# Splitting three multi-part steps of a merged attention and DeltaNet stage

## The reference, cut to what matters

```
# head group A, causal attention, 8 heads, then a norm over the 512 outputs of a token
s = qn . k_nope + qp . k_pe, scaled, causal mask
p = softmax(s)
o = p @ v ;  y_mla = o * rsqrt(mean(o*o) + EPS) * out_norm
# head group B, gated DeltaNet, 4 heads, chunked
lower  = strict_lower(k_beta @ k.T * decay)
sol    = triangular_solve(lower + I, [v_beta | k_beta * exp(g)])
a_qk   = causal(q @ k.T * decay)
v_new  = u_c - w_c @ state ; o_c = q_dec @ state + a_qk @ v_new
state  = state * exp(g_last) + k_dec.T @ v_new
```

## Time and profile before

| what | value |
|---|---|
| median of 3 runs | 2585.17 us (2581.58 to 2592.66) |
| the profiled execution, its own time | 2578.27 us |
| span in its trace | 2576.6 us |
| PE, PEld busy | 2331.9, 1339.2 us |
| DVE, ACT, POOL busy | 1074.2, 910.1, 392.4 us |
| mean granted TensorE clock | 0.949 of full speed |

### The profile page before, as it was taken

One profiled execution on the slowest core, in us unless ns is written; L12 is line 12 of the kernel. 1 busy time (PEld: TensorE's weight loads), 2 busy tenths in 40 slices (PEclk: granted clock), 3 DMA queues, 4 the chain that ended last, 5 costly groups with the idle time before them and its releaser, 6 DMA issues. The chain is left out here.

```text
span 2576.6 us, 47589 instructions
## 1 busy us (share of the span) xinstructions
PE 2331.9 (91%) x17494; PEld 1339.2 (52%) x17495; DVE 1074.2 (42%) x2440; ACT 910.1 (35%) x2283; POOL 392.4 (15%) x630
## 2 busy tenths in 40 slices
PE   6999999999688999999999999699985999999990
PEld 2545545455356666666666667355543444444440
DVE  2433334333345665665666566224345222222223
ACT  2263462734545554554545554111110011010112
POOL 1000000000110000000000010133321222222224
PEclk8999999999879999999999999899987999999995
DMA  9112121110353213121221112833321879999787
GB/s 335 72 65 70 52 78 54 56 54 32 107 141 105 75 53 94 56 82 49 80 69 65 51 33 95 294 126 111 131 90 33 238 193 307 273 323 303 225 237 287
DMA packets 187896, 334.49 MB, mean 130 GB/s; under 512 B 19724, under 2 KB 119719, under 8 KB 184503
## 3 DMA queue, kind: packets, MB, share of 16 engines
q1 hardware_dynamic: 173878, 281.51, 32.3%
q0 software_dynamic: 13824, 50.34, 8.1%
HBM read 242.36 MB, written 89.44 MB: 129 GB/s over the span
## 5 line engine op out<-in xcount | busy, mean ns | idle before, releaser
L706 PE MATMUL pV<-mod_rows_then_work,w_in_sb 128*128 128x512 f32 x768 | 341.3, 598 | 4.7 <-DMA w_in_sb<-in_w_in_dram 4.7
L2066 PE MATMUL hidden_ps<-w,keys_values_then_all 128*128 x752 | 331.5, 594 | 1.0 <-SPq L1938 1.0
L1140 ACT ACTIVATE probs<-scores,neg_max 128x512 f32<-128x512 f32 (+3 forms) x320 | 199.5, 624 | 345.6 <-DVE neg_max L1265 228.5
L1417 PE MATMUL scores<-keys_values_then_all,queries 96*128 96x512 f32 (+3 forms) x640 | 309.9, 567 | 7.2 <-DMA keys_values_then_all<-kp_d 7.2
L706 PEld LDWEIGHTS pV<-mod_rows_then_work,w_in_sb 128*128 128x128 f32 x768 | 145.0, 191 | 178.2 <-issue 177.5
L2066 PEld LDWEIGHTS hidden_ps<-w,keys_values_then_all 128*128 128x128 f32 x752 | 143.2, 191 | 181.5 <-issue 181.5
L1715 PE MATMUL out_ps<-keys_values_then_all 128*128 128x512 f32 x512 | 226.2, 600 | 2.5 <-ACT keys_values_then_all L1580 2.5
L1422 PE MATMUL bank<-ident,probs 128*128 128x128 f32 x1088 | 188.7, 290 | 7.0 <-ACT probs L1140 6.7
L1265 DVE TENSOR_REDUCE neg_max<-scores 128x1 f32<-128x512 f32 x192 | 132.2, 688 | 131.7 <-PE scores L1417 131.1
L1434 PE MATMUL outT_ps<-probs_T,keys_values_then_all 128*64 128x128 f32 x2176 | 160.0, 287 | 27.3 <-issue 23.1
L1996 ACT ACTIVATE keys_values_then_all<-hidden_ps 128x256 f32<-128x256 f32 x47 | 18.0, 384 | 455.5 <-PE hidden_ps L2066 455.5
(11 more groups left out here) (368 smaller groups left out, 3317.3 us busy)
## 6 DMA issues: line engine op xcount, KB each, us to landing
w<-in_w_dram SPq DMA_DIRECT2D x64, 1024.0 KB, 10.3
w_sb<-in_w_dram SPq DMA_DIRECT2D x32, 1024.0 KB, 14.4
w_mod_rows<-in_w_mod_dram SPq DMA_DIRECT2D x16, 1024.0 KB, 5.0
kqv<-qkv_d SPq DMA_DIRECT2D x16, 768.0 KB, 4.3
mod_rows_then_work<-in_w_mod_dram SPq DMA_DIRECT2D x4, 2048.0 KB, 14.9
x_in<-in_x_dram SPq DMA_DIRECT2D x16, 512.0 KB, 4.2
qkv_d<-l_out SPq DMA_DIRECT2D x32, 256.0 KB, 2.3
keys_values_then_all<-y_d SPq DMA_DIRECT2D x16, 512.0 KB, 4.9
```

The lines of the kernel that those rows point to most:

```text
L706: last = pe.matmul(pV[n % 2][:], win[:, k, QKV0 + c * P:QKV0 + (c + 1) * P], hT[:, s % 2, k, :], start=(k == 0), stop=(k == ND - 1))
L1140: act.activation(prob[:, e, 0:w].rearrange("p t k -> p (t k)"), pS[e][:, 0:w * P], ACT.Exp, scale=-1.0, bias=nmin[:, i % 2, h, b:b + 1], a ...
L1417: pe.matmul(pS[e][:, 0:w * P], qT[:, i % 2, slot(h)], kT[:, 4 * b:4 * b + w, slot(h), :], start=True, stop=True).then_inc(s_ready, 1)
L2066: last = pe.matmul(pH[par][:], xT[par][:, k], m.w13[:, ds(slot, 1), k].rearrange("p s n -> p (s n)"), start=(k == 0), stop=(k == ND - 1))
```

## The change

K's four parts on DVE and POOL become separate steps. Step K keeps the four operations that write `lt`. KA follows. U0 then makes `xt[:, 0]` directly from the diagonal blocks of `lt`, by four operations of 32 partitions in place of one of 128 on the compact copy, and then the first U. A new step KB has the compact copy and, on POOL, the other four masks. U0 cost 0.0 in the spacing and K with KA 1.7; now K, KA, U0 and KB cost 2.5.

B keeps the minimum and the gaps. Its exponential is step BX and its four last operations are step B2, placed in the next tile's first pair: BX behind the first head's X, B2 behind the second head's. A keeps the square (and POOL's part). The scaling and SP's store are step AS: one pair later where the next tile has more than 4 pairs, which is so for 12 of the 16 tiles, else directly behind A.

```
@@ mix_order: atoms
+            if i and (i, hp, b) == (i, 0, 0):
+                atoms.append((0.0, [(("BX", "B2")[e], i - 1, 0)]))
...
             atoms.append((0.0, [("B", i, 0)]))
+        if i and o == (AH // 2 if TILE[i] >= 4 else AH // 2 - 1):
+            atoms.append((0.0, [("AS", i - 1, 0)]))
+    atoms.append((0.0, [("BX", NT - 1, 0), ("B2", NT - 1, 0)]))
...
@@ mix_order: steps
-        steps += [(1.0, ("K", n)), (0.0, ("U0", n)), (0.7, ("KA", n))] * prep
+        steps += [(1.0, ("K", n)), (0.5, ("KA", n)), (0.5, ("U0", n)), (0.5, ("KB", n))] * prep
@@ SP
-                elif kind == "A":
+                elif kind == "AS":
                     wait(ya_ready, n + 1)
@@ POOL
-                elif kind == "K":
+                elif kind == "KB":
                     wait(ltb_ready, n + 1)
@@ ACT
-                elif kind == "B":
+                elif kind == "BX":
                     wait(gap_ready, n + 1)
...
                     act.activation(ya[:], att[:].rearrange("p h d -> p (h d)"), ACT.Square, accum_out=ass[:]).then_inc(asq_ready, 1)
+                elif kind == "AS":
                     wait(a_pow, 2 * n + 2)
@@ DVE
                 elif kind == "K":
                     wait(kk_ready, n + 1)
                     wait(em_ready, n + 1)
-                    wait(xt_ready, n)
                     wait(xw_ready, n * NLV)
...
                     last.then_inc(lt_ready, 1)
+                elif kind == "KB":
                     wait(lt_ready, n + 1)
+                    wait(xt_ready, n)
                     for q in quarter:
                         last = dve.tensor_copy(ltb[q], lt[q, :, q])
                     last.then_inc(ltb_ready, 1)
-                    wait(ltb_ready, n + 1)
-                    dve.tensor_tensor(xt[:, 0], ltb[:], mask_b[:, 0].unsqueeze(1).to_broadcast([P, GH, BL]), ALU.mult).then_inc(x0_ready, 1)
...
                 elif kind == "U0":
+                    wait(lt_ready, n + 1)
+                    for q in quarter:
+                        last = dve.tensor_tensor(xt[q, 0], lt[q, :, q], mask_b[q, 0].unsqueeze(1).to_broadcast([BL, GH, BL]), ALU.mult)
+                    last.then_inc(x0_ready, 1)
                     wait(x0_ready, n + 1)
...
+                elif kind == "B2":
+                    nb = TILE[n] // 4 + 1
                     wait(wexp_ready, n + 1)
```

More of the change, by code:

```diff
@@ L736, in mix_order @@
             atoms.append((0.0, [("B", i, 0)]))
+        if i and o == (AH // 2 if TILE[i] >= 4 else AH // 2 - 1):
+            atoms.append((0.0, [("AS", i - 1, 0)]))
+    atoms.append((0.0, [("BX", NT - 1, 0), ("B2", NT - 1, 0)]))
     for o in range(AH // 2):
         atoms.append((0.44, [("O", NT - 1, o)]))
-    atoms.append((0.0, [("A", NT - 1, 0)]))
+    atoms.append((0.0, [("A", NT - 1, 0), ("AS", NT - 1, 0)]))
     steps = []
@@ L760, in mix_order @@
         steps += [(0.9, ("Y", n, 6)), (0.5, ("WU", n, 6))] * prep
-    order = [("G", 0), ("K", 0), ("U0", 0), ("KA", 0), ("S", 0, 0), ("X", 0, 0), ("S", 0, 1), ("X", 0, 1)]
+    order = [("G", 0), ("K", 0), ("KA", 0), ("U0", 0), ("KB", 0), ("S", 0, 0), ("X", 0, 0), ("S", 0, 1), ("X", 0, 1)]
     steps = [(cost, step) for cost, step in steps if step not in order]
```

## The result

The changed kernel takes 2549.28 us (median of 6; 2543.02 to 2552.67) against 2587.46 for the kernel before beside it: ratio 0.9846, 95% interval 0.9832 to 0.9859. That is 38 us faster, where 14 had been forecast, and lies 1.3 us above the lower end of the range. The profiled execution has a span of 2543.2 us, against 2576.6.

What follows compares the result with a forecast made beforehand. PE was taken to wait on attention's round trip through in-order DVE and ACT queues, no engine being full. Terms -7.5 - 3.2 - 3.2 = -13.9 us, applied to the 2585.17 us median, gave 2571.3 us, range 2548 to 2592.

Steps and rivals of the forecast that it cites:

- What bounds the kernel: Merged stage, 909 us: no engine full by its own work; PE waits for attention's round trip through in-order DVE and ACT.
- Part A: Norm's scaling on ACT one pair later: six tiles in full, less a quarter, -7.5 us; bounds 0 and 20 us.
- Part B: Block weights on DVE: wait for ACT's small exponential nearly vanishes, 0.2 us a tile, -3.2 us; bounds 0 and 25.0.
- Part K: Gram step on DVE: earlier probs_T copy -8.0 us, longer second group +4.8, net -3.2; bounds -19 and +16 us.
- Spacing: DeltaNet steps weigh 18.25, not 17.45; inverse's round trips drawn closer, 2 us on 47.4 of waits, offset, set at zero.
- Most waits pass in full: Rival, merged stage: A 20, B 8 and K's first group 12 us, 40 us gained, 2545 us; chance 0.10.
- Absorbed: Rival: each removed wait uncovers another; half a gain at A, none at B and K, about 2581 us; chance 0.27.
- The slower rival: Gram step's longer second group delays row minima: +24 us against -8 from A and B, 2601 us; chance 0.13.

Runs made afterwards that it cites:

- extra copy behind the square: Changed kernel plus one unused 128x512 ACT copy directly behind the norm's square, 16 times: ratio 0.9890.
- extra matmuls: Kernel before plus unneeded PE matmuls where PE waits behind the norm, 12 tiles: 18 a tile, 2615.91 us; 6 a tile, 2592.5 us.
- the kernel where ACT still waits at the old place: Kernel before with only the norm's scaling one pair later, ACT still waiting for POOL's root directly behind the square: 2578.98 us, ratio 0.9947.
- the run with fewer extra matmuls: Kernel before plus 4 matmuls before V of the fifth pair and 2 before T of the sixth, in 12 tiles: 2592.5 us, ratio 1.0007.
- the old costs: Kernel before with only the Gram step split, K, KA, U0 and KB weighing 1.7 together in the spacing as before: 2566.71 us, ratio 0.9932.
- the spacing alone: Kernel before, nothing split, with K's cost in the spacing 1.5 and KA's 1.0 in place of 1.0 and 0.7: 2580.56 us, ratio 0.9966.

## Why the prediction was wrong, point by point

**What bounds the kernel** held. PE waits on attention's round trip, and what counts is which link stands behind what in an in-order queue.

**Part A is the step that failed.** The term read -7.5 us: six tiles in full, less a quarter for what PE waits for next. The mechanism, a backlog on ACT that ends at a load of PE, was right and its size was wrong: A alone brings 31 us, in company 21. I had two stretches, one that passed in full and one that didn't, and took half. The second of them, at the norm of 1101.8, is one of only two tiles of twelve that gain nothing: ten pass on 0.8 to 1.8 us each, 14.5 us of PE's idle time together, twice the term, and no next wait takes a quarter of it back. The term's upper bound, 20 us, is what A has in company; alone it has more than the ACT time it frees. The extra copy behind the square fits the full price (+11 us for 9.7), and the extra matmuls that PE took in for nothing show that the idle time is there.

**The clock** was missing from the sum altogether, and is likely most of the rest. In the kernel before, around the norm at 923.95, the granted clock was at its full level up to 929 and then fell from the upper of its two levels (2.4 GHz) to the lower (1.2 GHz) for most of the next 4 us. The same follows the norms at 969.1, 1171.8, 1331.2 and 1420.8, all of them tiles in which a load stood 2.0 to 3.3 us; behind the norm at 1036.0, where one stood 2.48 us, it didn't fall. The last row is the stretch behind the norm at 1171.8:

```profile
core 0: us, PE busy (x) PEld busy (x) DVE busy (x) ACT busy (x) POOL busy (x), PEclk, DMA share, GB/s
923.00:929.00 6.00, 3.56 (x43) 1.91 (x41) 3.68 (x10) 4.99 (x15) 1.63 (x3) 1.00 0.33 83
929.00:933.00 4.00, 4.00 (x31) 3.26 (x30) 0.11 (x1) 1.22 (x4) 0.00 (x0) 0.57 0.94 300
1175.00:1179.00 4.00, 4.00 (x19) 2.84 (x18) 1.45 (x3) 1.12 (x4) 0.00 (x0) 0.59 0.19 70
```

In the changed kernel the 9 to 11 us behind these five norms all have a granted clock of 1.00. At 929, PE's loads had stood 3.24 us ahead of the fall:

```profile
928.41 0.54 PEld L1364 LDWEIGHTS bank<-W_half,A_transposed 64*64 64x64 f32 x8 [3.24 <-issue]
929.01 1.52 PEld L1434 LDWEIGHTS outT_ps<-probs_T,keys_values_then_all 128*64 128x64 f32 x16
```

The same two groups of loads in the kernel with A alone:

```profile
923.11 0.54 PEld L1369 LDWEIGHTS bank<-W_half,A_transposed 64*64 64x64 f32 x8 [1.58 <-issue]
923.71 0.85 PEld L1439 LDWEIGHTS outT_ps<-probs_T,keys_values_then_all 128*64 128x64 f32 x16
```

V's 16 loads took 1.52 us behind the long wait and 0.85 us behind the shorter one. From 800 to 1560 us the mean granted clock is 0.97 before, 0.98 with A alone and 0.99 in the changed kernel. All kernels but the two with extra matmuls have the same 17,495 loads; with A's whole split they are busy 1329.6 to 1335.8 us (nine profiles, mean 1332.9), without it and with no matmuls added 1339.2 to 1345.3 (eight, mean 1342.3), and with the extra copy behind the square 1338.8. The first line is that of the kernel with A alone, the second that of the kernel where ACT still waits at the old place:

```profile
PE 2324.6 (91%) x17494; PEld 1335.1 (52%) x17495; DVE 1074.2 (42%) x2440; ACT 908.5 (36%) x2283; POOL 392.3 (15%) x630
```

```profile
PE 2335.2 (91%) x17494; PEld 1343.9 (52%) x17495; DVE 1074.7 (42%) x2440; ACT 910.2 (35%) x2283; POOL 393.6 (15%) x630
```

The means lie 9 us apart. Over whole runs the mean granted clock was 0.944 to 0.951 in the kernel before and 0.952 to 0.957 with A alone, measured beside it. So it is shown that the clock is higher with A, which changes no instruction of PE. How much of the 31 us is idle time and how much is clock is worked out from profiles, not shown by a run: the run with fewer extra matmuls was meant to, and left the clock where it was. The one pair of profiles, 20 us apart, has 16 us less idle and 4.5 us less load time in the stage.

**Part B** was -3.2 us; alone it is -6 (-2 to -10 by the interval), in company nothing. The reasoning held (DVE waits while it has little else).

**Part K** was -8.0 + 4.8 = -3.2 us. Alone it is -16, in company about -7.5. This net is too small as well. Where it was read, at chunk 7, the copy came 0.8 us sooner against my 0.5, and the second group took 2.15 us as predicted (2.1). Sixteen times 0.8 is 13 us, so even with nothing paid the 16 to 18 us aren't explained. Which waits the split shortens isn't shown: with the old costs the idle of T's and V's loads is 77.6 and 73.5 us, hardly less than the 78.5 and 74.4 before, in a profile of that kernel's slowest run (2583.68 us). Whether the 0.3 us a chunk that I let reach PE did so stays open too. The four products took 1.16 us here, not my 1.0, and U 0.29 us each time with no long ones left. DVE's busy time rose by 9.5 us, not by only a few. The Trainium skill's figure for four products (VectorE: DVE Perf Modes, The TRN2 errata) was the closer one, and its rule on two SBUF inputs (SBUF — State Buffer, Who interferes with whom) fits:

```profile
L1210 DVE TENSOR_TENSOR W_U_blocks<-block_ident,X_transposed x16: 292/292/295, 708.9 to 1517.9; 128x128 f32<-128x128 f32 x16
```

**Spacing** was put at zero. Alone it is -9 us, beside K's split nothing. It didn't draw the inverse's round trips closer at no cost: with the spacing alone the two waits of the inverse are 27.1 and 24.8 us, together 4.5 us more than the 47.4 before, where I had put 2.

**The rivals.** "Most waits pass in full" (2545 us, chance 0.10) is what happened, with A as its largest part as written there, nothing from B in it, and the clock, which it didn't have. "Absorbed" is what B did beside A and K. The slower rival had its group of 2.15 us, but no run with K's split was slower than the kernel before. Its -8 us from A and B were also less than the 10.7 us of my own two terms.

**Open:** why A and B, or A and K, give less together than apart (31 + 6 + 16 = 53 us, 40 together by the ratio); the runs show that they overlap, not which idle stretch is claimed twice. Also where the 16 to 18 us of K's split and the 9 us of the spacing lie in the trace.

## What to carry to other kernels

Before sizing a wait on an in-order engine, follow its queue behind the wait in every instance, not in two, up to the first instruction that PE waits for. Where ACT worked up to there without a stop, half to all of the wait and the operation reached PE here, whichever step PE was waiting for (eight of twelve tiles); where it stopped 3 us for something else first, nothing did, and where it stopped 1 to 2 us, part did. Moving the operation behind that link brought as much as taking it off the engine. An operation whose input comes from another engine by a detour (a root on POOL) belongs a few steps behind the one that starts the detour. Long idle stretches of PE can cost more than their length, since the granted clock fell behind five of these norms; so a few long waits deserve attention ahead of as much time in short ones. And parts that are measured alone can't be added up.

## What the runs showed of the hardware that was not expected

The granted clock of a stretch changed with an edit that touches neither PE's instructions nor their order: A alone took it from 0.97 to 0.98 of full speed from 800 to 1560 us, and over all profiles the same loads took 9 us less with A than without. On DVE, four multiplications of 32 partitions and 128 elements, one behind the other, took 1.16 us, while one of 128 partitions and as many elements took 0.29 us: what counted here was the number of instructions, not the partitions. POOL scaled 128x512 in 1.58 us, ACT in 0.73 us.
